# A hybrid decoder step on one core: the first half of w_out loaded in one go, one more weight unit split early, and the order of matmuls around the last attention output changed

## The reference, cut to what matters

```python
def merge_and_mlp(x, o, pool_out, w_out, g_mlp, w_up, w_down):
    mix = jnp.concatenate([o.reshape(B, T, ATTN_WIDTH), pool_out], axis=-1)
    h = x + mix @ w_out
    a = jnp.square(jax.nn.relu(rms_norm(h, g_mlp) @ w_up))
    return h + a @ w_down
```

## Time and profile before

| | us |
|---|---|
| median of 3 runs | 894.92 (893.73, 894.92, 901.22) |
| the profiled execution, its own time | 892.73 |
| span in its profile, first to last instruction | 890.9 |
| what lies around the span (892.73 less 890.9) | 1.83 |
| mean granted PE clock, share of full speed | 0.968 |

### The profile page before, as it was taken

One profiled execution on the slowest core, in us unless ns is written; L12 is line 12 of the kernel. 1 busy time (PEld: TensorE's weight loads), 2 busy tenths in 40 slices (PEclk: granted clock), 3 DMA queues, 4 the chain that ended last, 5 costly groups with the idle time before them and its releaser, 6 DMA issues.

```text
span 890.9 us, 18225 instructions
## 1 busy us (share of the span) xinstructions
PE 819.0 (92%) x7776; PEld 747.1 (84%) x7776; DVE 429.2 (48%) x800; ACT 345.5 (39%) x643; POOL 139.4 (16%) x166
## 2 busy tenths in 40 slices
PE   5999999997888867777999999999999999999997
PEld 4999987775555644557999999999999999999996
DVE  5434646664655476675237342334233433244554
ACT  6511155553466564563235331133212331033432
POOL 0001101100685336620220000000000000000122
PEclk8999999998899988999999999999999999999998
DMA  8922628852461115524522112222221122222222
GB/s 304 313 88 96 194 55 251 256 194 96 120 209 53 36 49 197 209 95 113 173 95 94 49 48 93 94 94 94 94 89 36 64 94 94 95 95 94 96 95 107
DMA packets 51946, 107.22 MB, mean 120 GB/s; under 512 B 7579, under 2 KB 21295, under 8 KB 49582
## 3 DMA queue, kind: packets, MB, share of 16 engines
q1 hardware_dynamic: 44973, 72.80, 24.7%
q0 software_dynamic: 6912, 33.56, 11.0%
HBM read 101.95 MB, written 8.53 MB: 124 GB/s over the span
## 4 chain that ended last, share of the span: by engine, by line
PE 55%; POOL 2%; DMA 2%; issue 2%; DVE 2%; ACT 1%; SPq 0%; DVEq 0%; ACTq 0%; POOLq 0%
PE banks L1856 45%; PE banks L2147 5%; DMA low<-in_w_out 1%; PE banks L1668 1%; POOL zone L1439 1%; DMA low<-in_cache_slc,idx_slc 1%; DMA zone<-in_cache_slc,idx_slc 1%; PE banks L1736 1%; POOL zone L349 1%; POOL low L349 1%; PE banks L2157 0%; POOL rowsT L1439 0%; PE banks L1709 0%; PE banks L1687 0%; ACT xh L1862 0%
## 5 line engine op out<-in xcount | busy, mean ns | idle before, releaser
L1856 PE MATMUL banks<-xh,wh 128*128 128x288 f32 x640 | 137.9, 297 | 5.0 <-DVE wl L1841 2.5
L1856 PE MATMUL banks<-xl,wh 128*128 128x288 f32 x640 | 137.6, 297 | 0.0
L1856 PE MATMUL banks<-xh,wl 128*128 128x288 f32 x640 | 137.5, 296 | 0.0
L1836 ACT ACTIVATE wh<-low 128x1024 fp32r<-128x1024 f32 x79 | 82.4, 1050 | 112.7 <-PE banks L1856 102.8
L1856 PEld LDWEIGHTS banks<-xh,wh 128*128 128x128 f32 x640 | 103.4, 189 | 6.0 <-issue 3.2
L1856 PEld LDWEIGHTS banks<-xl,wh 128*128 128x128 f32 x640 | 103.7, 190 | 0.0
L1856 PEld LDWEIGHTS banks<-xh,wl 128*128 128x128 f32 x640 | 103.6, 190 | 0.0
L1841 DVE TENSOR_TENSOR wl<-low,wh 128x1024 fp32r<-128x1024 f32 x80 | 97.1, 1215 | 4.6 <-ACT wh L1836 4.6
L1856 PE MATMUL banks<-al,wh 128*128 128x288 f32 x384 | 82.3, 296 | 0.0
L1856 PE MATMUL banks<-ah,wl 128*128 128x288 f32 x384 | 82.3, 296 | 0.0
L1856 PE MATMUL banks<-ah,wh 128*128 128x288 f32 x384 | 82.2, 296 | 0.0
(11 more groups left out here) (349 smaller groups left out, 1563.0 us busy)
## 6 DMA issues: line engine op xcount, KB each, us to landing
low<-in_w_down SPq DMA_DIRECT2D x10, 2048.0 KB, 7.8
low<-in_w_up SPq DMA_DIRECT2D x8, 2048.0 KB, 8.3
zone<-in_cmp_w SPq DMA_DIRECT2D x16, 256.0 KB, 4.3
o_swin<-in_state_win SPq DMA_DIRECT2D x8, 504.0 KB
px<-in_x_prompt SPq DMA_DIRECT2D x4, 512.0 KB, 5.1
u_raw<-in_w_in SPq DMA_DIRECT2D x1, 2048.0 KB, 10.2
q_raw<-in_w_in SPq DMA_DIRECT2D x1, 2048.0 KB, 10.6
low<-in_state_win SPq DMA_DIRECT2D x4, 512.0 KB, 4.2
```

Source lines behind the costliest of these rows:

```text
L1836: act.activation(wcols(m.wh, i), raw_cols(i), ACT.Copy).then_inc(wh_ready, 1)
L1856: last = pe.matmul(out(i, hf), w[wi], half(x[:, k, :], hf), start=first and part == 0, stop=end and part == 2)
```

## The change

- `w_out`, columns 0 to 511, is issued in one go after `v_done` 17: columns 0 to 127 under `first_in`, 128 to 255 under a new semaphore `second_in`, 256 to 511 under `ring_in[0]`. The wait for `v_done` 24 is gone. Three more DMAs are issued (nine in place of six).
- ACT splits `wh` of unit 1 in `ending.scalar`, behind `wh` of unit 0 and ahead of `keep_output(3)`, after a wait for `second_in`. `split(1)` goes from its list in `mlp`.
- DVE does `split(1)` ahead of the attention blocks of xl instead of behind them.
- PE does three pooling products of unit 0, then `turn_output(3)`, then the fourth, then waits for `wl_ready` 2 and does the four pooling products of unit 1; unit 0's attention products follow, then unit 1's.
- The ring slots 1 and 3 of the split weights change places in memory.

```diff
--- before.py
+++ after.py
@@ -314,7 +314,7 @@
     first, zone = a["rowsT"], a["zone"]
     work = zone + WORK - LOW
     m.xh, m.xl = sb("xh", a["qT"] - 4 * TOK, [P, KT_D, TOK], F32R), sb("xl", work + 1152, [P, KT_D, TOK], F32R)
-    slots = ((work + 7744, work + 8768), (first + 8312, zone + 9216), (work, work + 5760), (a["kT"], a["kT"] + 1024))
+    slots = ((work + 7744, work + 8768), (a["kT"], a["kT"] + 1024), (work, work + 5760), (first + 8312, zone + 9216))
     m.wh = [sb(f"wh{r}", at, [P, KT_D * P], F32R) for r, (at, _) in enumerate(slots)]
     m.wl = [sb(f"wl{r}", at, [P, KT_D * P], F32R) for r, (_, at) in enumerate(slots)]
     m.ah, m.al = sb("ah", zone, [P, KT_D, TOK], F32R), sb("al", zone + 4608, [P, KT_D, TOK], F32R)
@@ -1422,8 +1422,8 @@
                 load_window(sp, m, 2 * (n % 2) + e, 2 * n + e, sems)
         sp.wait_ge(v_done, VN * (NPAIR - 2) + X)
         load_w_out(sp, m, sems.first_in, 0, 0, P)
-        sp.wait_ge(v_done, VN * NPAIR)
-        load_w_out(sp, m, sems.ring_in[0], 0, P, 512)
+        load_w_out(sp, m, sems.second_in, 0, P, 2 * P)
+        load_w_out(sp, m, sems.ring_in[0], 0, 2 * P, 512)
 
     def on_gpsimd(pool):
         for n in range(NPAIR):
@@ -1775,6 +1775,7 @@
                         turn_output(n - 2)
         ending.tensor(pe)
         turn_output(NPAIR - 1)
+        ending.tensor_rest(pe)
 
     return on_sync, on_gpsimd, on_scalar, on_vector, on_tensor
 
@@ -1868,18 +1869,28 @@
     def early_scalar(act):
         act.wait_ge(sems.first_in, 48)
         act.activation(wcols(m.wh, 0), raw_cols(0), ACT.Copy).then_inc(wh_ready, 1)
+        act.wait_ge(sems.second_in, 48)
+        act.activation(wcols(m.wh, 1), raw_cols(1), ACT.Copy).then_inc(wh_ready, 1)
 
     def early_vector(dve):
         split_low(dve, 0, 0)
 
     def early_tensor(pe):
         pe.wait_ge(wl_ready, 1)
-        for c in range(4):
+        for c in range(3):
             pe.wait_ge(xl_ready, c + 1)
             product(pe, 0, MIX_ORDER[c], m.xh, m.xl, c == 0, False)
 
+    def early_tensor_rest(pe):
+        pe.wait_ge(xl_ready, 4)
+        product(pe, 0, MIX_ORDER[3], m.xh, m.xl, False, False)
+        pe.wait_ge(wl_ready, 2)
+        for c in range(4):
+            product(pe, 1, MIX_ORDER[c], m.xh, m.xl, c == 0, False)
+
     ending.mix_scalar, ending.mix_vector = mix_scalar, mix_vector
     ending.scalar, ending.vector, ending.tensor = early_scalar, early_vector, early_tensor
+    ending.tensor_rest = early_tensor_rest
 
     def on_sync(sp):
         sp.wait_ge(wl_ready, 2)
@@ -1931,7 +1942,6 @@
         for k in MIX_ORDER[4:]:
             act.activation(m.xh[:, k, :], m.mixT[:, k, :], ACT.Copy).then_inc(xh_ready, 1)
         act.wait_ge(sems.ring_in[0], W0)
-        split(1)
         split(2)
         for n in range(FIRST):
             if n:
@@ -1997,9 +2007,9 @@
         def split(i, base=0):
             split_low(dve, i, base)
 
+        split(1)
         for c in range(4, KT_D):
             low_mix(dve, c)
-        split(1)
         for n in range(FIRST):
             split(n + 2)
             dve.wait_ge(unit_mm, n + 1)
@@ -2105,7 +2115,7 @@
             if n >= 2:
                 pe.wait_ge(kept, n - 1)
             for c, k in enumerate(MIX_ORDER):
-                if n == 0 and c < 4:
+                if n < 2 and c < 4:
                     continue
                 if n == 0:
                     pe.wait_ge(xl_ready, c + 1)
@@ -2249,6 +2259,7 @@
         sems.slc_in = [[sem(f"slc_in{q}_{x}") for x in range(4)] for q in range(2)]
         sems.win_in = [sem("win_in0"), sem("win_in1")]
         sems.ring_in, sems.first_in = [sem("ring_in0"), sem("ring_in1")], sem("first_in")
+        sems.second_in = sem("second_in")
         place_attention(nc, m)
         place_project(nc, m)
         m.imp_g = m.spX[:, 0:96]
```

## The result

| | before | changed |
|---|---|---|
| median of 20 executions each | 895.05 us | 890.0 us (874.37 to 894.72) |
| repeat, 35 and 12 executions | 895.66 | 890.53, ratio 0.995 (0.9928 to 0.9972) |
| second repeat, 32 and 12 | 896.31 | 890.7, ratio 0.9955 (0.9927 to 0.9982) |
| the profiled execution, its span | 890.9 | 885.3 |

The comparison made first gave a ratio of 0.9876 (0.9837 to 0.9915), 11 us. It rests on 4 of the 20 executions only, since one of them, at 874.37 us, sets the bar under which the others of that kernel count as undisturbed. All 20 against all 20 give 890.0 / 895.05 = 0.9944, 5.05 us, and the medians of the two repeats lie 5.1 and 5.6 us apart. Taken together, the medians are 890.2 us (44 executions of the changed kernel) and 895.6 (87 of the kernel before), 5.4 us or 0.6% apart.

The account below looks back on a forecast made before the run. PE bounds the kernel, losing time only at the sample to mlp boundary: gaps 2.14 + 2.00, clock 1.64, tails and restarts 0.37, together 6.15 us; 894.3 less 6.15 gives 888.2 us, range 885.8 to 891.5.

Parts of the forecast that it names:

- The gaps: PE standstills at the boundary of sample and mlp: 2.14 us waiting for xl, 2.00 us for unit 1's wl, both closed.
- the sum: Work left on PE from unit 0's first matmul to unit 2's: 24 pairs per unit, transpose and restart, together 12.95 us.
- Each cover: Slack hiding moved work: ACT 5 us, or 1.8 by the bound; DVE 1.1 us; SP's added DMAs in waiting time.
- less 0.8 for the spread of single runs: Low end of the range: profiled time less the gain, 886.6, less 0.8 for scatter, giving 885.8 us.
- Against 425.67 that is 6.15 us.: Boundary: without gaps or clock drop unit 2 starts at 419.5 instead of 425.67, a gain of 6.15 us.
- I take it that the clock doesn't fall: Between 406.54 and 419.5 PE has no standstill, so the half-clock loss of 1.64 us counts as gained.
- Rival A: Clock falls all the same, later or elsewhere in the stretch; 1.64 us stay, 889.8 us; chance 0.16.
- The paragraph on SP's issues: SP's three added DMAs take 1.87 us of issue time; second_in should land near 402.9, by the bound 406.5.
- B: First load of w_out held up by those queued behind it; gain 2.25 to 5.75, at worst 892.0 us; chance 0.07.
- C: ACT's new wait for second_in holds keep_output(3) and PE if it lands after 408.3; at worst 894.9 us; chance 0.03.
- D: Another wait fills the gaps; one of about 2 us stays with a clock drop, 891.8 us; chance 0.06.
- even sharing: If the 2 MB share DMA engines evenly, first_in lands at 408.1, wh of unit 0 starts 3.9 us late; gain 2.25.

Follow-up runs that it names:

- e1: Kernel before with only the load moved: columns 128 to 511 of w_out issued straight behind the first 128; 897.7 us beside 895.66, ratio 1.0032.
- e2: Kernel before with only the last output turned behind three pooling products instead of four; 894.73 us beside 895.66, ratio 0.9993.
- e3: Changed kernel without unit 1's four pooling products ahead of unit 0's attention products; 893.07 us beside 895.66, ratio 0.9972.
- e4: Changed kernel with ACT waiting for ring_in[0], thus all of the load, ahead of unit 0; 895.84 us beside 894.05, ratio 1.0014.
- e5: Changed kernel with DVE's split(1) back behind the four attention blocks of xl; 895.37 us beside 894.69, ratio 1.0024.
- e6: Kernel before with only columns 128 to 255 of w_out loaded early, the rest behind pair 3; 894.96 us beside 894.69, ratio 0.9996.
- e8: Kernel before with an extra early 1.5 MB load of w_out that nothing uses; 898.01 us beside 894.69, ratio 1.0031.
- e9: Kernel before with unused matmuls, 14 behind the turn and 13 between units 0 and 1; 895.46 us beside 894.05, ratio 1.0019.
- e12: Changed kernel with unused matmuls filling standstills ahead of the boundary: 18 and 15 ahead of pairs 2 and 3, 6 in pair 3; 887.39 us beside 896.31, ratio 0.9917.
- e7: Changed kernel with the load of columns 256 to 511 put back behind the end of pair 3; 891.59 us beside 894.69, ratio 0.9939.
- e10: Changed kernel with 20, 20 and 10 unused matmuls in the standstills ahead of the boundary; 888.16 us beside 894.05, ratio 0.9931.
- e13: Changed kernel with e12's unused matmuls and columns 256 to 511 loaded behind the end of pair 3; 889.26 us beside 896.31, ratio 0.9931.

## Why the prediction was right and wrong

*The gaps.* Right in place and size. 19.13 us to unit 2 became 13.00; the sum had 12.95. Each cover held: ACT's (5.47 us idle left), DVE's (1.22), SP's. e1, e2 and e3 show that the parts work only together: the turn alone wins nothing, the load alone loses, and without unit 1 ahead 1.34 us of standstill stay.

*The step that failed: "less 0.8 for the spread of single runs".* This term made the low end of the range, 886.6 - 0.8 = 885.8, and with it only a chance of 0.12 for a time under 886.0. The comparison made first stands for 0.9876 x 895.05 = 884.0 us, below that end. The spread was far larger than 0.8: the 44 executions of the changed kernel have a standard deviation of 3.7 us and run from 874.37 to 895.97, the 87 of the kernel before have 2.8 us. I had read it off three runs and a profile. The 884.0 needs no mechanism of the kernel: two repeats don't have it, and it rests on four executions with a very fast one among them.

The medians of all executions, 890.0, 890.5 and 890.7, lie inside 885.8 to 891.5. That they stand 2 us above the forecast of 888.2 is in the main the base: I took 894.3 for the kernel before from four executions, and 87 have 895.6.

*"Against 425.67 that is 6.15 us."* Right as the size of the boundary: 19.13 - 13.00 = 6.13 in the profile. The whole came out at 5.4 us, 0.7 less, but the intervals of the repeats include 6.15, so a shortfall isn't shown.

*"I take it that the clock doesn't fall", 1.64 us counted as gained.* This held in the stretch that it speaks of. In the seven profiles with a standstill of 2 us or more at the boundary or just ahead of it (before, e1, e2, e4, e5, e6, e8) the clock fell behind at least one of them, though not behind each; in the ten others it was 1.00 from the first product to unit 2. What the term left out is the clock ahead of the boundary. Two of three profiles of the changed kernel have a fall in pair 3, which costs 1.5 us up to the first product (11.45 against 9.92). Rival A, to which I had given 0.16, comes nearest to it, but spoke of falls in the stretch only. But the kernel before can have that fall too (11.46 in e9; 9.92 and 9.93 in before and e2), so it is a loss of the change only if the change makes it likelier, which is open. The step from one profile's clock to the mean of the executions should have been two chances of this fall, one for each kernel.

*The step that was missing.* The paragraph on SP's issues asked whether the transfers land in time, and not what they hold up. The traffic holds up PE inside pair 3, by all that can be seen for its own instructions: 3.98 us in e1, 2.73 in e8, 0.80 in one profile of the changed kernel. In the kernel before, the small row of q8 at this place would have told of a block under way. The changed kernel pays 0.3 us for it in that profile; it can cost 3.7 us at the first product (13.60 - 9.92), as the same 1.5 MB in other parts do in e1. Why 1.5 MB in rows of 384 columns hurt more than 0.5 MB in rows of 128 and 1 MB in rows of 256 wasn't tried.

*B, C and D.* `first_in` was 0.7 us later, hidden. C's wait occurred in some profiles (1.02 us in the second repeat, 1.81 in e5, where `wh` of unit 1 starts 9.6 us behind the issue of `first_in`), and ACT hid it each time. Their prices hold up: waiting for all of the load costs 3.93 us at the first product (3.9 in the prediction's even sharing), and a late `wl` of unit 1 holds PE for 4.39.

*Where the scatter comes from.* Over the 44 executions of the changed kernel the time falls as the mean granted clock rises (correlation -0.82). Much of it lies ahead of `first_in`, where e1 and e5 run the same code: e1's profile issues it at 401.96 and e5's at 394.67. Their busy time from 100 to 200 us:

```profile
100.00:200.00 100.00, 90.90 (x1212) 76.48 (x1212) 55.66 (x106) 47.17 (x104) 11.61 (x13) 0.95 0.64 197
```
```profile
100.00:200.00 100.00, 92.11 (x1307) 78.27 (x1307) 58.67 (x112) 50.07 (x111) 11.71 (x13) 1.00 0.64 197
```

With a clock of 0.95 in place of 1.00 PE gets through 1212 matmuls in this time and not 1307.

*Left open:* whether the early traffic makes the fall in pair 3 likelier (it is there in 6 of 11 profiles with early traffic and nothing filled in ahead of pair 3, and in 1 of 3 without early traffic, too few to tell); whether the added matmuls of e12 win anything over the changed kernel; and what PE waits for in the standstills that name only "issue", since no view shows an instruction fetch being asked for.

## What to carry to other kernels

When a standstill is closed by an earlier transfer, look at what else uses the DMA engines at that time; the instruction queue counts. A profile shows the clock of one execution: where it falls behind a gap that you close, ask how often executions have that fall, and where else one can stand in either kernel. And measure a change under 1% by many executions of both kernels, and take the width of a forecast from many too: here a ratio from four of them was off by as much as the effect.

## What the runs showed of the hardware that I had not expected

- PE stood still for 3.98 (e1), 2.73 (e8), 0.80 (the changed kernel's second repeat) and 0.27 us (e7), always between the same two matmuls, with early loads of `w_out` beside it. The row of such a standstill names no engine, only "issue"; each time a block of the instruction queue had landed 1.5 to 3.5 us before PE went on. That PE waited for its instructions is inferred from this.
- With unused matmuls of 128 columns in f32 in the gaps, 0.24 us each, the granted clock was 1.00 from 350 us to the end of pair 3 in all three profiles that have them (e10, e12, e13); the three of the changed kernel have 0.84, 0.92 and 0.92 from 350 to 394 us.
- In profiles of one code the granted clock fell at different places, and the point where unit 0's weights are issued moved by up to 12 us (394.67 in e5 to 406.61 in e7).
